# GpSimd writes the scaled states of a tile in one product; start, first norm and last tile rearranged, in a two-layer hybrid decoder step

## The chip, the cores and the metric

The program runs on all 8 cores of one Trainium2 chip, each with its own prompt (2048 tokens) and 16 sample tokens; the weights are the same on each and no core waits for another. The metric is device microseconds of the slowest core.

## What is computed

Per token x (1024 channels), layer by layer, in float32 with bf16 matmul operands:

```
even: h = rmsnorm(x); u,q,f,i,g = h @ w_in          # 256 | 6 heads x 128 each
      pool: mean over 2/4/8/16 tokens - u, per-group linear, scale
      head: k = 1-f, v = silu(i), S_t = diag(f_t) S_(t-1) + k_t outer v_t, o_t = S_t^T q_t
            o = rmsnorm(o) * gain * sigmoid(g)
      x += concat(pool, o) @ w_out
odd:  h = rmsnorm(x); b,c,z = h @ w_in
      x += (b * conv3(c * z)) @ w_out
each: x += relu(rmsnorm(x) @ w1)^2 @ w2              # 4096 wide
end:  y = rmsnorm(x)
```

Outputs are y for the prompt and the samples, and the new states. The recurrence runs by chunks of 128 tokens: with the decay of a chunk as a column, the state before chunk j is scaled by cc[:, j], cast to bf16 and multiplied by the decayed q; a masked product inside the chunk is added.

## The kernel before

Channels lie on partitions, tokens along the free dimension. The 2064 tokens go in two halves (0 to 1023, 1024 to 2063); a half is cut into tiles for the heads (HT: 512 tokens) and for the dense part (DT: 512 in the first half, 352, 352 and 336 in the second). Weights come from DRAM as float32 and are cast to bf16 by the DMA into a ring of six slots of 4096 columns; GpSimd issues these loads (g_load, two DMAs of 2048 columns a unit). x, outputs and states are moved by SyncE's queue.

The program is written as Python generators (g_...), one for each piece of work. A list scheduler (Sched) takes, among the operations that the generators offer, the one with the lowest estimated start plus a small weight times its priority, and appends it to its engine's instruction stream. So the order on each engine is fixed when the program is built; at run time the engines only wait on semaphores. PRI holds the priorities by name, DMA_RATE the transfer speeds that the estimates use. The numbers of the scheduler change only the order.

The pieces that matter here:
- g_x0 loads the first half of x: tile 0 in two parts of 256 columns, two DMAs each, then, when the weights of head 1 have landed, tile 1. Head 0's weights wait for tile 0's second part, head 2's for a part of tile 1.
- g_norm: eight squares (ScalarE), seven adds (VectorE or GpSimd, seng), a matmul with ones (float32, passes=4), Ln and Exp (ScalarE), and eight products into hT (VectorE). With final=True the products go to pages and each is sent out by one DMA (two where the sample tokens are in it).
- g_x1 loads the second half's x for the heads into mixT, used as a staging area, after the first half's fronts.
- g_front(h, t): projections f, i, g of head h on tile t, with their sigmoids. Weights lie as kc * 512 + r * 128 (q, f, i, g). g_back(h, t): log decay, its scan (VectorE), the exponentials, q projection, transposes, the masked product, then the state steps. The last are:

```
for j in range(nj):
    yield ACT(Spb[j], Vin, AF.Copy, ..., scale=cc[:, j:j + 1])       # scaled state, bf16
    yield STT(Vout, Vin, cc[:, j:j + 1], bank(kd_)[j], mult, add)    # V_(j+1) = cc_j V_j + K_j
    yield MMG([(bank(ko)[j], Spb[j], qd[j]), (bank(ko)[j], vtok[j], sm[j])])
    Vin = Vout
```

- g_pools: the pooling mixer, one of whose tiles has adds on GpSimd.
- g_outproj, g_ff1, g_ff2, g_conv: the dense part. The dense part of the first half runs interleaved with the heads of the second half. g_ff2 in its last pair spawns the norm of the next layer, or the final one.
- Each GpSimd tensor product also writes B_poolser, so they run one after the other.

In the profile, L494 is ACT, L514 tensor_tensor (TT), L529 scalar_tensor_tensor (STT), L549 matmul groups, L558 transposes, L564 DMA issue.

## Time and profile before

| | |
|---|---|
| median of three runs | 1538.13 us (1537.94 to 1538.3) |
| profiled execution | 1537.33 us |
| span of its slowest core | 1535.8 us |
| spans of all cores | 1529.1 to 1535.8 us |
| granted TensorE clock, mean | 0.984 |
| TensorE busy | 1455.6 us (95%) |
| VectorE, ScalarE, GpSimd busy | 887.7 (58%), 632.0 (41%), 186.0 us (12%) |
| moved by DMA | 138.56 MB, mean 90 GB/s |

The profile is of the slowest core. "Busy" counts the union of an engine's instructions; the granted clock of a stretch is 1.00 at 2.4 GHz and 0.50 at 1.2 GHz. A releaser ("<-DVE arena L514") is the instruction whose end let a waiting one go. Names as arena, ring, hT, mixT, x_sb are SBUF tensors, pp a PSUM bank. A DMA row of a queue gives packets, megabytes written and the share of 16 DMA engines' time; q0 is GpSimd's queue, q1 SyncE's.

### The profile page before, as it was taken

How to read it: one execution, taken by the hardware profiler on the slowest of the kernel's cores; microseconds unless marked ns; L12 is line 12 of the kernel's file. 1: busy time of each engine (PE TensorE's matmuls, PEld its weight loads, DVE VectorE, ACT ScalarE, POOL GpSimd, SP SyncE). 2: the span in 40 equal slices, each digit the busy share in tenths (PEclk: the TensorE clock that was granted, in tenths of full speed). 3: DMA queues.
4: the chain of work that ended last, by engine and by line, in shares of the span. 5: the costliest groups of instructions: out<-in, count | busy, mean ns of one | idle time of the engine just before them, and what ended most of it. 6: DMA issues, size and time to landing. Idle time of an engine off the chain costs nothing.

```text
span 1535.8 us, 24078 instructions; the slowest of 8 cores (1529.1 to 1535.8 us)
## 1 busy us (share of the span) xinstructions
PE 1455.6 (95%) x9034; PEld 817.6 (53%) x9034; DVE 887.7 (58%) x1860; ACT 632.0 (41%) x1187; POOL 186.0 (12%) x272
## 2 busy tenths in 40 slices
PE   2789799999999999999999999999999999999996
PEld 1445344554555444444444446666666666666663
DVE  4766686676657768565333368533357767433355
ACT  3788747655797433222212234222133224211132
POOL 1233313001111141100100010001001110001000
PEclk9899799999999999999999999999999999999998
DMA  6835333157346646962633558055245544155222
GB/s 142 183 56 83 56 56 85 28 114 166 83 85 140 152 70 99 174 117 52 110 56 61 104 111 167 15 97 85 51 72 83 95 89 83 25 86 95 52 58 75
DMA packets 49553, 138.56 MB, mean 90 GB/s; under 512 B 7840, under 2 KB 15904, under 8 KB 47904
## 3 DMA queue, kind: packets, MB, share of 16 engines
q0 software_dynamic: 29408, 101.76, 39.9%
q1 hardware_dynamic: 19600, 34.93, 6.9%
q8 instruction: 75, 1.23, 0.3%
q10 hardware_dynamic: 432, 0.33, 0.1%
q14 instruction: 38, 0.31, 0.1%
HBM read 223.21 MB, written 15.54 MB: 155 GB/s over the span
## 4 chain that ended last, share of the span: by engine, by line
PE 90%; ACT 4%; DVE 3%; DMA 1%; issue 1%; POOL 0%; DVEq 0%; SPq 0%; ACTq 0%; POOLq 0%
PE pp L549 89%; ACT arena L494 3%; DVE hT L529 1%; ACT L494 1%; DVE arena L514 1%; DMA x_sb<-xp 1%; DMA ring<-wst 1%; DVE arena L529 0%; POOL arena L514 0%; PE pp L558 0%; DVE arena L542 0%; DVE x_sb L514 0%; ACT mixT L494 0%; DVE mixT L514 0%; DVE mixT L529 0%
## 5 line engine op out<-in xcount | busy, mean ns | idle before, releaser
L549 PE MATMUL pp<-hT,ring 128*128 128x512 bf16 (+3 forms) x4320 | 785.5, 339 | 5.4 <-DVE hT L529 4.5
L549 PEld LDWEIGHTS pp<-hT,ring 128*128 128x128 bf16 x4320 | 408.5, 98 | 346.6 <-issue 24.9
L549 PE MATMUL pp<-mixT,ring 128*128 128x512 bf16 (+2 forms) x3200 | 576.0, 339 | 7.5 <-DVE mixT L514 4.5
L549 PEld LDWEIGHTS pp<-mixT,ring 128*128 128x128 bf16 x3200 | 311.4, 98 | 249.8 <-issue 17.1
L494 ACT ACTIVATE mixT<-pp 128x512 bf16<-128x512 f32 (+2 forms) x320 | 164.6, 514 | 485.2 <-PE pp L549 484.3
L514 DVE TENSOR_TENSOR x_sb<-x_sb,pp 128x512 f32<-128x512 f32 (+3 forms) x384 | 220.7, 579 | 199.0 <-PE pp L549 198.6
L514 DVE TENSOR_TENSOR mixT<-mixT 128x512 bf16<-128x512 bf16 (+2 forms) x320 | 119.3, 376 | 234.8 <-ACT mixT L494 233.9
L564 POOL DMA_DIRECT2D ring<-wst x202 | 107.7, 542 | 971.0 <-PE pp L549 957.2
L494 ACT ACTIVATE arena<-pp 128x512 f32<-128x512 f32 (+9 forms) x261 | 129.2, 508 | 160.2 <-PE pp L549 142.7
L494 ACT ACTIVATE arena<-x_sb 128x512 f32<-128x512 f32 (+3 forms) x184 | 97.6, 538 | 156.7 <-DVE x_sb L514 144.3
L514 DVE TENSOR_TENSOR arena<-arena 128x512 f32<-128x512 f32 (+6 forms) x195 | 114.3, 586 | 23.6 <-ACT arena L494 19.6
L514 DVE TENSOR_TENSOR arena<-pp,arena 128x512 bf16<-128x512 f32 (+5 forms) x124 | 75.2, 610 | 76.7 <-ACT arena L494 48.6
L514 POOL TENSOR_TENSOR arena<-arena 128x512 f32<-128x512 f32 (+5 forms) x62 | 76.4, 1232 | 295.8 <-ACT arena L494 116.0
L494 ACT ACT_TABLE_LOAD x71 | 91.1, 1283 | 4.6 <-issue 2.5
L529 DVE SCALAR_TENSOR_TENSOR hT<-x_sb,cst_s,arena 128x512 bf16<-128x512 f32 (+3 forms) x144 | 84.9, 655 | 11.6 <-ACT arena L494 11.6
L494 ACT ACTIVATE arena<-arena 128x512 f32<-128x512 f32 (+3 forms) x128 | 73.0, 585 | 11.3 <-PE pp L549 5.0
L549 PE MATMUL pp<-arena 128*128 128x128 bf16 (+2 forms) x504 | 59.2, 225 | 14.5 <-ACT arena L494 12.0
L529 DVE SCALAR_TENSOR_TENSOR arena<-arena,cst_s 128x512 f32<-128x512 f32 (+4 forms) x88 | 53.2, 608 | 23.1 <-ACT arena L494 21.7
L549 PEld LDWEIGHTS pp<-arena 128*128 128x128 bf16 (+1 forms) x504 | 36.2, 100 | 46.9 <-issue 32.6
L549 PEld LDWEIGHTS pp<-ring,hT 128*128 128x128 bf16 (+1 forms) x816 | 47.7, 98 | 6.8 <-issue 2.9
L549 PE MATMUL pp<-ring,hT 128*128 128x128 bf16 (+1 forms) x816 | 50.5, 220 | 0.0
L494 ACT ACTIVATE arena<-arena,cst_s 128x512 f32<-128x512 f32 (+2 forms) x40 | 25.3, 636 | 57.8 <-DVE arena L514 57.8
(65 smaller groups left out, 426.1 us busy)
## 6 DMA issues: line engine op xcount, KB each, us to landing
ring<-wst POOLq DMA_DIRECT2D x186, 512.0 KB, 9.0
arena<-st_hgrn SPq DMA_DIRECT2D x6, 1024.0 KB, 5.3
nhs<-arena SPq DMA_DIRECT2D x6, 1024.0 KB, 7.4
x_sb<-xp SPq DMA_DIRECT2D x8, 512.0 KB, 10.7
mixT<-xp SPq DMA_DIRECT2D x8, 512.0 KB, 7.8
ring<-wst POOLq DMA_DIRECT2D x16, 256.0 KB, 7.9
yp<-arena SPq DMA_DIRECT2D x16, 256.0 KB, 10.2
yp<-arena SPq DMA_DIRECT2D x16, 176.0 KB, 1.9
```

Source lines behind the costliest of these rows:

```text
L494: return e.activation(out=out, in_=in_, func=func, bias=bias, scale=scale)
L514: return Op(eng, lambda e: e.tensor_tensor(out=out, in0=in0, in1=in1, op=op), R, W, occ=d, dur=d)
L529: return Op("dve", lambda e: e.scalar_tensor_tensor(out=out, in0=in0, scalar=scalar, in1=in1, op0=op0, op1=op1), R, W, occ=d, dur=d)
L549: ins = e.matmul(o, l, r, start=s, stop=t)
L564: fns = [(lambda e, o=o, i=i: e.dma_start(out=o, in_=i, **kw)) for (o, i) in pairs]
```

## The change

1. State steps: the four ScalarE casts become two GpSimd products, one for chunk 0 and one for chunks 1 to 3 behind the third step; the eight matmuls stand together after all four steps.
2. Loads at the start: no gate on any weight load; tile 0's x from a second copy (xp0) in which four channels of 256 tokens are contiguous; head 0's weights in four DMAs of 1024 columns, each with its own buffer name and semaphore; the weights of a head are laid out by projection (f, i, g, q, 1024 columns each). g_x1's loads wait for head 5's weights.
3. First norm (g_normx): tile 0's two parts have a norm of their own. Three of the eight products go ScalarE copy, then GpSimd product; the sum over channels is partly done by accumulating matmuls. Tile 1's adds go to GpSimd. Front (0, 0) runs its projections by half tiles, the first of them chunk by chunk.
4. Last tile: in the last pair of the last g_ff2 the tile of 336 columns is cut at 1952 into 224 and 112. Both get g_norm_tail: adds for channels 1 to 5 only, three squares straight to the matmul, three products on GpSimd, and outputs in four DMAs of two channels, for the last on two queues, and one for the samples.
5. Writes into mixT by second-half heads and pooling wait for the norm of tile 3. "poolp" is set after the sample part.
6. New priorities, seed and DMA rates. JIT is 0, so the seed has no effect.

```
-    PRI = {'norma': 0, 'frontA': 4.6, 'add': 8.7, 'pools': 10.8, 'normy': 59.0, 'cchain': 18.7, 'normc': 0, 'normz': 4.2, 'poolA': 3.1}
-    DMA_RATE = {"sp": 200e3, "act": 200e3, "pool": 270e3}
+    PRI = {'norma': 0, 'frontA': 12.9, 'add': 12.3, 'pools': 10.8, 'normy': 65.5, 'cchain': 17.8, 'normc': 0, 'normz': 18.0, 'poolA': 9.8, 'normp': 12.3, 'poolB': 10.5, 'normb': 7.4, 'relu': 0, 'backB': 20.4}
+    DMA_RATE = {"sp": 300e3, "act": 200e3, "pool": 300e3}
...
+                st = 1024 if key == ("H", 0, 0) else 2048
+                for c0 in range(0, unit_cols[u], st):
...
+                if key[0] == "H":
+                    for i, pr in enumerate(pairs):
+                        k = st // 1024
+                        if key == ("H", 0, 5):
+                            gate_x1.extend(B_ring[s])
+                        yield DMA("pool", ring_ds[s][i * k], [pr], after_, B_ring[s][i * k:(i + 1) * k], nbytes=st * 512)
...
-                        extra = [B_ring[loaded[("H", 0, 1)]]] if t == 1 and q == 0 else []
...
-                if t == 0:
-                    yield WAIT(("ld", ("H", 0, 1)))
...
+                        src = xp0[:, i, cs, :] if t == 0 else xp[:, cs, u:v]
...
+                    if t == 0:
+                        S.spawn(g_normx(u, v), 0, f"normp{u}")
+                    else:
+                        S.spawn(g_norm(0, u, v, *xloc(0, u, v), seng="pool"), 5, f"normx{u}")
...
+        def g_normx(a, b):
...
+            else:
+                for c in range(8):
+                    s_, Bs_ = sq[c % 4]
+                    yield ACT(s_, xap(c), AF.Square, xbf(c), Bs_)
+                    yield MMG([(bank(pk)[:, 0:N], onesf, s_, c == 0, c == 7)], Bs_ + [B_const], [B_ps[pk]], passes=4)
...
+            nx = 3
+            for c in range(nx):
+                yield ACT(xg[c][0], xap(7 - c), AF.Copy, xbf(7 - c) + [B_const], xg[c][1], scale=gcols[:, 7 - c:8 - c])
...
+                if c < nx:
+                    yield TT(hT[:, 7 - c, a:b], xg[c][0], rs, ALU.mult, xg[c][1] + Br, bh(7 - c, a, b), eng="pool")
...
+            yield TT(Spb3[:, 0:1, :], Vc[:, h:h + 1, :], cc3[:, 0:1, :], ALU.mult, [B_V[h]] + Bcc + Blf[0][1:], BSpj[0], eng="pool")
             Vin, BVin = Vc[:, h, :], [B_V[h]]
             for j in range(nj):
                 Vout, BVout = (V3[:, j, :], BVj[j]) if j < nj - 1 else (Vc[:, h, :], [B_V[h]])
-                yield ACT(Spb[:, j * 128:(j + 1) * 128], Vin, AF.Copy, BVin + Bcc + Blf[0][1:], BSpj[j], scale=cc[:, j:j + 1])
                 yield STT(Vout, Vin, cc[:, j:j + 1], bank(kd_)[:, j * 128:(j + 1) * 128], ALU.mult, ALU.add,
                           BVin + Bcc + [B_ps[kd_]] + BG, BVout)
+                Vin, BVin = Vout, BVout
+                if j == nj - 2:
+                    yield TT(Spb3[:, 1:nj, :], V3[:, 0:nj - 1, :], cc3[:, 1:nj, :], ALU.mult, BVj + BG + Bcc, BSpj[1:], eng="pool")
+            for j in range(nj):
                 yield MMG([...])
...
+            if T0 >= SPLIT:
+                yield WAIT(("hT", 0, HT[1][-1][0]))
...
+                tiles = [(a, a, b) for (a, b) in DT[half]]
+                if last and n_after == 4 and half == 1:
+                    ta, tb = DT[1][-1]
+                    tiles[-1:] = [(ta, ta, TCUT), (ta, TCUT, tb)]
...
+            for i, cs in enumerate(((0, 1), (4, 5), (2, 3), (6, 7))):
+                yield DMA(("sp", "act")[i % 2 if b > NT else 0], y_ds[y_ptr[0] % len(y_ds)],
+                          [(yp[:, cs[0]:cs[1] + 1, a:a + e], yo[:, cs[0]:cs[1] + 1, 0:e])], [BO[c] for c in cs], (), nbytes=e * 1024)
...
-        S.spawn(g_load(head_seq(0), Q_HEAD, {("H", 0, 0): (("xl", sum(HT[0][0]) // 2, 0), bx(0, sum(HT[0][0]) // 2, HT[0][0][1])), ("H", 0, 2): (("xl", HT[0][1][0], 1), bx(2, *HT[0][1]))}), 40, "hload")
+        S.spawn(g_load(head_seq(0), Q_HEAD), 40, "hload")
```

## Rows read from the trace of the kernel before

**Rows 1.** The page, part 4: shares of the chain that ended last, by line.

```profile
PE pp L549 89%; ACT arena L494 3%; DVE hT L529 1%; ACT L494 1%; DVE arena L514 1%; DMA x_sb<-xp 1%; DMA ring<-wst 1%; DVE arena L529 0%; POOL arena L514 0%; PE pp L558 0%; DVE arena L542 0%; DVE x_sb L514 0%; ACT mixT L494 0%; DVE mixT L514 0%; DVE mixT L529 0%
```

**Rows 2.** Busy time by stage: start:end, length, busy (x instructions), granted clock, DMA share, GB/s.

```profile
0.00:29.86 29.86, 2.38 (x4) 1.03 (x5) 15.23 (x52) 10.04 (x23) 4.56 (x12) 1.00 0.75 147
...
41.00:60.00 19.00, 12.23 (x53) 5.22 (x51) 12.47 (x23) 15.57 (x28) 5.93 (x9) 0.73 0.99 225
60.00:107.00 47.00, 38.97 (x324) 23.06 (x323) 34.24 (x75) 38.88 (x68) 13.37 (x14) 0.99 0.51 86
107.00:188.00 81.00, 66.75 (x502) 37.45 (x501) 56.39 (x118) 69.33 (x127) 23.47 (x26) 0.88 0.43 66
...
258.00:276.00 18.00, 14.23 (x79) 7.06 (x78) 12.85 (x30) 11.78 (x27) 3.62 (x6) 0.81 0.75 117
276.00:530.00 254.00, 253.08 (x1774) 130.89 (x1773) 167.67 (x345) 167.75 (x310) 26.17 (x39) 1.00 0.48 105
...
1511.70:1521.05 9.35, 9.28 (x64) 6.19 (x64) 6.53 (x14) 3.38 (x7) 0.00 (x0) 1.00 0.22 81
1521.05:1535.80 14.75, 0.80 (x2) 0.30 (x2) 5.36 (x11) 1.42 (x3) 0.00 (x0) 0.68 0.30 93
```

**Rows 3.** Chain, then timeline, 0 to 62 us: start, length, engine, line, operation.

```profile
1.57 11.50 DMA x_sb<-xp
...
18.34 3.25 DVE L529 SCALAR_TENSOR_TENSOR hT<-x_sb,cst_s,arena 128x256 bf16<-128x256 f32 x8
...
26.46 3.25 DVE L529 SCALAR_TENSOR_TENSOR hT<-x_sb,cst_s,arena 128x256 bf16<-128x256 f32 x8 [2.41 <-ACT arena L494]
...
29.86 3.57 PE L549 MATMUL pp<-hT,ring 128*128 128x512 bf16 x8 [4.48 <-DVE hT L529]
...
39.14 1.95 PE L549 MATMUL pp<-ring,hT 128*128 128x128 bf16 x32
...
59.70 0.99 DVE L529 SCALAR_TENSOR_TENSOR hT<-x_sb,cst_s,arena 128x512 bf16<-128x512 f32 x1
```

**Rows 4.** DMA queues in 16:29, 36:46, 903.1:911.1, 607.6:610.3, 676.8:678.2: packets, MB, share.

```profile
q0 software_dynamic: 468, 1.72, 89.0%
...
q1 hardware_dynamic: 1759, 3.39, 92.7%
...
q0 software_dynamic: 275, 1.00, 81.1%
q1 hardware_dynamic: 344, 0.65, 22.8%
...
q0 software_dynamic: 115, 0.33, 81.6%
q1 hardware_dynamic: 146, 0.13, 15.2%
...
q0 software_dynamic: 39, 0.14, 47.9%
q1 hardware_dynamic: 437, 0.12, 38.8%
```

**Rows 5.** GpSimd on arena tiles, whole span: ns min/median/max, first and last.

```profile
L514 POOL TENSOR_TENSOR arena<-arena x62: 1038/1087/2372, 43.5 to 570.8; 128x512 f32<-128x512 f32 x38, 128x526 f32<-128x526 f32 x8, 64x524 f32<-64x524 f32 x4, 128x524 f32<-128x524 f32 x4
```

**Rows 6.** ScalarE, 41 to 188: casts by form; TensorE waiting for it (us, times).

```profile
L494 ACT ACTIVATE arena<-arena,gsm 128x128 bf16<-128x128 f32 x36 | 13.2, 394 | 2.2 <-DVE arena L529 2.1
...
L494 ACT ACTIVATE arena<-Vc,gsm 128x128 bf16<-128x128 f32 x12 | 4.6, 396 | 0.0
...
  PE pp L549: 16.1, 25
```

**Rows 7.** The chain that ended last, 236 to 290 us.

```profile
258.94 11.15 DMA ring<-wst
```

**Rows 8.** Timeline from 1490 us: the last tile's output.

```profile
1524.86 3.92 DVE L529 SCALAR_TENSOR_TENSOR arena<-x_sb,cst_s,arena 128x336 f32<-128x336 f32 x8 [2.16 <-ACT arena L494]
...
1532.73 0.43 SPq L564 DMA_DIRECT2D ys<-arena  x1
```

More of the change, by code:

```diff
@@ L352, in build @@
     xp = din("xp", [128, 8, NT])
+    xp0 = din("xp0", [128, 2, 8, 256])
     xs = din("xs", [128, 8 * NSMP])
@@ L462, in bm @@
             return [Bm_[c][i] for i in segs(TB, a, b)]
-        B_ring = [Buf(f"ring{i}") for i in range(NSLOT)]
+        B_ring = [[Buf(f"ring{i}_{q}") for q in range(4)] for i in range(NSLOT)]
         B_pg = [[Buf(f"pg{i}lo"), Buf(f"pg{i}hi")] for i in range(NPAGE + NOV)]
@@ L655, in g_norm @@
             N = b - a
+            if final and b >= (TCUT if TCUT else NTOK):
+                yield from g_norm_tail(n, a, b, xap, xbf, seng)
+                return
             pA, pS, pT = yield GRAB(1, 1, 1)
@@ L836, in g_front @@
             yield ACT(s1, bank(kf)[:, 0:L], AF.Sigmoid, [B_ps[kf]], Bs1, scale=-1.0)
             hput(kf)
-            (ki,) = yield from htake(half)
-            yield MMG([(bank(ki)[:, j * 128:(j + 1) * 128], hT[:, kc, T0 + j * 128:T0 + (j + 1) * 128], Wt(kc, 256, 384),
-                        kc == 0, kc == 7) for j in range(nj) for kc in range(8)], Rw, [B_ps[ki]])
+            if first:
+                yield proji(ki, Tm, T1, [B_ps[ki], Bx2[ki][1]])
+            else:
+                (ki,) = yield from htake(half)
+                yield proji(ki, T0, T1, [B_ps[ki]])
@@ L844, in g_front @@
             PAGES.put(p3)
-            (kg,) = yield from htake(half)
-            yield MMG([(bank(kg)[:, 0:L], Wt(kc, 384, 512), hT[:, kc, tk], kc == 0, kc == 7) for kc in range(8)], Rw, [B_ps[kg]])
+            if first:
+                yield proj(kg, 2, Tm, T1, [B_ps[kg], Bx2[kg][1]])
+            else:
+                (kg,) = yield from htake(half)
+                yield proj(kg, 2, T0, T1, [B_ps[kg]])
             yield ACT(sg, bank(kg)[:, 0:L], AF.Sigmoid, [B_ps[kg]], Bsg)
```

161 lines of the change are left out of this document (128 added, 33 removed).

## Prediction

> **What bounds the kernel now.** I began with the chain of waits [rows 1]: 89% of the span is TensorE in the one helper that records matmuls, so only time in which TensorE has nothing to do, or works at its lower clock, can be won. The second view is the table of busy time by stage [rows 2]. The reader should subtract TensorE's busy time from each stretch: 27.5 us idle before 29.86, 6.8 in 41 to 60, 8.0 in 60 to 107, 14.3 in 107 to 188, 3.8 in 258 to 276, 0.9 in 276 to 530, 14.0 after 1521.05. These seven make 75.3 of the 80.2 us that TensorE idles in all; the dense work between has nothing to give. The granted clock tells the rest: 0.73 in 41 to 60, 0.88 in 107 to 188, 0.81 in 258 to 276; each fall follows a stretch with gaps. So three places matter: the start, the first half's heads (41 to 188), the end.
>
> **The start: loads.** In before, the first x tile (columns 0 to 511, 2 MB) comes alone; the weights of head 0 wait for it. The critical chain has the second x piece landing at 1.57 + 11.50 = 13.1 us; the first hT chunk begins at 18.34 (5.3 us after it), the second half's eight chunks run 26.46 to 29.71, and the first projection starts at 29.86 [rows 3]. After, every load is issued at once: SyncE sends x tile 0, then x tile 1; GpSimd sends six slots (heads 0 to 4 and pooling), 13 DMAs, with no gate. How 16 DMA engines share between the queues decides. Ring loads alone move 132 GB/s (1.72 MB in 13 us) at a share of 0.89, so 150 GB/s of bf16 at full share [rows 4]: a head (1.05 MB) is 7.0 us of all engines, the six slots 5.8 MB or 38 us. Where both queues were full, 344 packets of 2 KB went beside 275 ring packets, 1.25 to 1 [rows 4]. Pieces of 896 B, strided at both ends, went 146 to 115, or 1.27 to 1. But 64-byte pieces cut from a contiguous source row of 512 B went with 39 ring packets at 437 in all, some 11 to 1 [rows 4]: a turn seems to be a contiguous source run. The new input xp0 makes the source run 4 KB while SBUF is still written in 1 KB pieces, so I take four pieces a turn.
>
> Bounds for x tile 0 (2048 pieces; alone it needs about 8 us of all engines, an estimate: 2.1 MB at some 260 GB/s, between the 147 GB/s of the first stretch in rows 2 and the 339 GB/s of 2 KB pieces in rows 4). At four to one it meets 512 ring packets, just head 0: 8 + 7 = 15 us, landed at about 17. At 1.27 to one it meets 1613 of the 1664: 8 + 37 = 45, landed at about 47. I take the first, since the 64-byte row has the same shape.
>
> The new first norm has the same chain (5.3 us), with five chunks on VectorE and three products on GpSimd instead of eight on VectorE. First half: 1024 pieces beside 256 ring packets, 4 + 3.5 us, landed about 11 with latency, first chunk 16, and TensorE does projections f, i, g of half the tile meanwhile. Second half: landed 17, first chunk 22 to 23, last 25. Against 29.86 this is 5 us, and another 3 for half of the three projections done early (the first eight matmuls take 3.57 us, [rows 3]; three such projections 7 to 10), 8 in all. But then x tile 1 is late next. It follows on the same queue with 2 KB pieces, at 1.25 to one: 1024 pieces beside some 820 ring packets (3.4 MB, 22 us) plus 6 us of its own (2.1 MB at 339 GB/s, [rows 4]) lands about 17 + 28 = 45 to 50. Its norm adds, moved to GpSimd, cost 1.09 us each (GpSimd's median, [rows 5]), in a chain behind the squares: hT of tile 1 from about 56, against 59.70 [rows 3]. So the 8 us shrink to 3. I count -3, with ends -9 (x tile 1 lands early) and +6 (the second end of the sharing, half hidden because the work of tile 1 then follows without a gap).
>
> **State casts.** Per head and tile, before: four ScalarE casts of 128x128 between the state steps; they are 36 + 12 in the first half's heads at 0.39 us, 13.2 + 4.6 = 17.8 us [rows 6]. After: one GpSimd product of 128 columns, one of 384 behind the third step. ScalarE is busy 15.6 of 19, 38.9 of 47 and 69.3 of 81 us [rows 2], 84% of 41 to 188, and TensorE waits 16.1 us, 25 times, for a ScalarE tile there [rows 6], of 29.1 us idle (55%). Upper end: the stretch follows ScalarE, -17.8. Lower end: nothing is freed on the path, and the longer chain is open 12 times. Its length: before, the last cast stands behind step three with 0.39 us; after, the 384-column product does and lasts, by width from 1.04 us (the shortest of 512 columns, [rows 5]), 0.8 us, up to 1.8 by the longest (2.37). I take 1.0, since the median is near the shortest; less the 0.39 of the cast that it replaces, 0.6 us: 12 x 0.6 = +7. My value: 55% of 17.8 = -9.8, plus 0.6 for each of the last two heads, behind which nothing is queued: about -9. Part of this is clock: fewer gaps in 107 to 188, where 0.88 was granted. In the second half, 12 more pairs of products stand beside dense matmuls, with TensorE idle 0.9 us in 254 [rows 2]: cost 0; with the cover gone, +7.
>
> The products wait on VectorE's step, on an in-order queue, and ring loads stand behind them. Before shows what that costs: a load issued only at 258.9, in the middle of norm adds, landed 11.15 us later and was the chain [rows 7], in the stretch with 3.8 us idle and a clock of 0.81, some 6 us in all (14.2 busy x 0.19 = 2.7, plus 3.8). The new priorities reorder this place too, either way: 0, with ends -6 and +6. Of x half 2, moved behind head 5's load, the mixT writes wait for the norm by an explicit WAIT; its readers start beyond 270, so 0.
>
> The Trainium skill's page "SBUF — State Buffer", section "Who interferes with whom", speaks against this change: a VectorE instruction with two SBUF inputs and a GpSimd one that reads SBUF exclude each other for a whole instruction. The trace agrees so far as that equal products on GpSimd take 1.04 to 2.37 us [rows 5]. By it each of the first half's 12 wide products could wait one VectorE instruction of 0.7 us more (an estimate), the whole sum 8 us smaller: 1527, the end of the likeliest case's own range.
>
> **The end.** Before, from 1521.05: add, square, sum, matmul, Ln, Exp to 1524.86; eight chunks, 3.92 us; SyncE issues sixteen DMAs, the last at 1532.73 [rows 8]; 14.75 us in all. After, the last tile is cut at 1952 into 224 and 112 columns. TensorE: 64 matmuls at 336 columns take 9.28 us [rows 2], 145 ns each. 128-column ones take 1.95/32 = 61 ns [rows 3], floor for 112; 224 by width is 98 ns. 64 x (61 + 98) = 10.2, so +0.9. Behind the last matmul, at 112 columns: add 0.3, square 0.35 and matmul 0.4 (the last three squares go to TensorE directly), Ln and Exp 0.8, then five chunks of some 0.27 beside three on GpSimd 1.3, issue 1.0 on two queues, landing 2.5: 6.7. VectorE's backlog from the 224 columns (16 adds, 5 chunks in 3.9 us of matmul) adds some 1.2. 14.75 - 0.9 - 7.9 = -6. Ends: -8 (no backlog), -4 (the two queues land one after the other).
>
> **Sum.** -3 - 9 + 0 - 6 = -18. The profiled run took 1537.3 (span 1535.8 plus 1.5), 0.8 below the median of 1538.1. So 1519.5. The likeliest case's own range: 1511 to 1527.
>
> **Rivals.**
> A. GpSimd takes ScalarE's place. TensorE waits as long for the 384-column product as it did for the casts, so 41 to 188 keeps its length. For it: the chain really is longer, and one wait gates all eight matmuls. Against it: those waits were ScalarE's queue, not only one cast. 1537.3 - 3 + 2 - 6 = 1530.
> B. Head and clock both give. With fewer gaps the clock never falls in 107 to 188 (66.8 busy x 0.12 = 8 us back), x tile 1 lands by 40 (-9). 6 of those 8 beyond the 9 counted: 1537.3 - 9 - 9 - 6 - 6 = 1507. Against: tile 1 needs DMA time that the weights take.
> C. Slower: x starves. If the turn is one 1 KB piece, x tile 0 lands about 47, all second-half chunks at 54 instead of 29.71, +24, less 3 for early projections. Nothing hides it, TensorE has only the first half's projections. 1537.3 + 21 - 9 - 6 = 1543. It decides once more than about 1400 of the 1664 ring packets go ahead of x tile 0's last piece. For it: 2 KB and 896 B rows; against: the 64-byte row. The Trainium skill's page "DMA: Bandwidth & Descriptors", section "Queues, rings and completion order", says that each engine switches queues at packet boundaries and that a packet holds many descriptors; this trace's 2 KB and 896 B rows look like single pieces, and the measurement decides.
> D. It doesn't do what it says: order shifts eat the gain in the heads and only the end is won, with loads held behind GpSimd products: 1537.3 - 6 + 6 = 1537.
>
> **How the numbers follow.** Forecast 0.56, A 0.19, B 0.13, C 0.07, D 0.05. The range reaches from just below B's 1507 to between A and D, and leaves out C, D and what of B lies lower, some 0.17: 1505 to 1536. A measurement of this kernel tells about 0.2%, 3 us. Faster by more: forecast, B, A and a little of D, 0.88; same 0.04; slower 0.08.
>
> **What would show it.** First projection between 15 and 18 us, second half of the tile by 24: the sharing is right; at 45, C. hT of tile 1 from 54 to 58. ScalarE busy in the first heads down by some 18 us, its row of 128x128 casts gone, TensorE's waits for ScalarE in 41 to 188 below 8 us and those for GpSimd below 6 us; above 12, A. The stage that ends at 188 in rows 2 ends about 176. GpSimd's 384-column product near 0.8 to 1.0 us. No new wait on a ring load over 3 us. From last matmul to the end 7 to 9 us. I am wrong if GpSimd's queue holds loads, or if the new order opens gaps between 276 and 1150, of which before shows none.

## The result, and the profile after

The changed kernel takes 1558.78 us (median, 1557.98 to 1561.38) against 1538.22: a ratio of 1.0135, 95% interval 1.0122 to 1.0147, so 20.6 us slower. The forecast was 1519.5, and the range ended at 1536. In some runs, of the kernel before too, a pair of cores or half of the chip shows a lower granted clock than the rest; such runs are left out (e17's interval has one, and with theirs e9 would be at 1560.4 and e12 at 1567.3), and of e1 to e4, where it was so every time, only the other four cores are used.

The page of the kernel after (core 2, span 1556.4 us; in before TensorE was busy as long, 1455.6 us, and the same line had 89% of the chain [rows 1]):

```profile
PE 1455.5 (94%) x9052; PEld 828.2 (53%) x9140; DVE 894.2 (57%) x1851; ACT 604.4 (39%) x1111; POOL 239.0 (15%) x346
...
PE pp L551 84%; DMA x_sb<-xp 3%; ACT arena L496 3%; DMA ring<-wst 2%; ACT L496 2%; SPq L566 1%; DVE arena L516 1%; DVE arena L531 1%; POOL arena L516 1%; DVE hT L531 0%; PE pp L560 0%; ACT mixT L496 0%; DVE mixT L531 0%; POOL ring L566 0%; DVE arena L544 0%
...
x_sb<-xp SPq DMA_DIRECT2D x8, 512.0 KB, 31.2
```

The chain gives DMA 3 and 2% of the span, and the median DMA of x (eight of 512 KB) takes 31.2 us from issue to landing. The stages of core 2, with the columns of [rows 2]:

```profile
0.00:29.86 29.86, 6.61 (x18) 3.73 (x18) 9.81 (x35) 6.78 (x17) 11.66 (x24) 0.94 0.94 180
41.00:60.00 19.00, 0.40 (x1) 0.00 (x0) 4.88 (x5) 5.21 (x11) 7.09 (x7) 0.50 0.69 146
60.00:107.00 47.00, 42.62 (x329) 25.36 (x335) 32.30 (x64) 39.33 (x56) 16.48 (x19) 0.92 0.27 52
107.00:188.00 81.00, 68.31 (x547) 41.28 (x554) 55.27 (x118) 71.04 (x104) 30.47 (x38) 0.92 0.38 63
276.00:530.00 254.00, 246.52 (x1578) 125.85 (x1603) 143.58 (x283) 114.16 (x208) 34.67 (x53) 1.00 0.46 93
```

TensorE idles 23.3 us before 29.86 (27.5 in before), 18.6 in 41 to 60 (6.8), 7.5 in 276 to 530 (0.9). Between the last two the order differs too much to compare by the clock, so I count from the residual adds, of which the first 384 (of 416, of 424 where the last tile is cut) are the same in both kernels; the first marks the start of the first outproj. A stage's loss is TensorE's idle time plus its busy time times (1 - the clock granted while it was busy).

| stage (adds) | before, core 4 | after, core 2 | after, core 4 |
|---|---|---|---|
| start to first add | 191.5, loss 68.7 | 202.0, loss 83.8 | 200.8, loss 82.3 |
| to the 17th | 82.3, 6.4 | 85.2, 7.0 | 83.5, 5.3 |
| to the 113th | 493.9, 2.3 | 509.4, 16.2 | 499.7, 6.8 |
| to the 384th | 678.6, 2.6 | 673.7, 3.2 | 673.7, 3.2 |
| to the end | 89.5 | 86.1 | 84.9 |

So the start loses 10 us where 12 were to be won, and 12 to 16 more go between 290 and 800 us on one core of each pair (0 and 1, 2 and 3, ...), 6 to 7 on the other. The other core is 8 to 14 us faster in every run: the medians are 1553.9 and 1543.6, against 1535.4 and 1530.5 in before. TensorE's waits for ring loads, core 2 and then core 3 (us in all, times, longest), and a piece of core 2's chain:

```profile
PE pp L551 <- DMA ring<-wst: 6.5, 3, 3.8
```

```profile
PE pp L551 <- DMA ring<-wst: 1.3, 2, 1.0
```

```profile
411.84 0.59 POOL ring L566
412.43 20.25 DMA ring<-wst
```

**The start, as it ran.** DMA queues of core 2 from 12 to 32 us (packets, MB, share), the longest piece of its chain before 400 us, then its timeline; a bracket gives the idle time before and what ended it:

```profile
q0 software_dynamic: 1142, 2.51, 75.8%
q1 hardware_dynamic: 1137, 1.29, 27.2%
```

```profile
14.14 43.01 DMA x_sb<-xp
```

```profile
1.07 14.95 SPq L566 DMA_DIRECT2D x_sb<-xp  x8
...
20.79 0.42 PE L551 MATMUL pp<-hT,ring 128*128 128x256 bf16 x1
...
30.30 1.03 ACT L496 ACTIVATE arena<-x_sb 128x256 f32<-128x256 f32 x3 [9.72 <-DMA x_sb<-xp]
...
53.80 0.63 ACT L496 ACTIVATE arena<-x_sb 128x512 f32<-128x512 f32 x1 [5.39 <-DMA x_sb<-xp]
54.33 0.40 ACT L496 ACTIVATE arena<-arena 128x256 f32<-128x256 f32 x1
...
54.77 4.88 DVE L531 SCALAR_TENSOR_TENSOR hT<-x_sb,cst_s,arena 128x256 bf16<-128x256 f32 x5 [34.62 <-ACT arena L496]
...
60.92 2.04 PE L551 MATMUL pp<-arena,cst_s 128*128 128x512 f32 x2 [19.52 <-POOL arena L516]
...
63.34 1.86 PE L551 MATMUL pp<-hT,ring 128*128 128x256 bf16 x8 [0.37 <-POOL hT L516]
```

The two queues went packet for packet, 1142 to 1137. Not all of these are large: counted by size in the trace from 12 us to the landing of x tile 0 at 30.2, GpSimd's queue has 1081 packets, 675 of them ring loads (2 or 4 KB written), 256 of the pooling weights (128 B) and 150 of 4 B, and SyncE's has 1080, of which 946 are x tile 0's pieces of 1 KB and 102 tile 1's of 2 KB. Cores 4 and 5 have 1102 to 1098 and 1104 to 1103. x tile 0's four DMAs landed at 6.3, 12.2, 19.2 and 30.2 us (10.3 to 16.0 in before), x tile 1 at 57.1 (44.8 in before; 45 to 50 in the forecast). That last one is the piece of 43.01 us in the chain. The first matmul on half of tile 0 is at 20.79. The second half's square runs at 30.30 as soon as x is there, but its hT begins at 54.77: ScalarE's queue has the squares of tile 1 ahead of the second half's last two steps, and the Exp (54.33) stands behind a square that waited for x tile 1 (53.80). VectorE waited 34.62 us for it. TensorE has tile 1's sum of squares ahead of its projections (19.52 us of wait), and GpSimd's three products end only at 63.2, so it goes on at 63.34. In before tile 0's hT was complete at 29.7. Tile 1's hT begins at 64.5, against 59.7 in before.

### The profile page after: what moved, and what is told of

Its sections match the earlier page's. It is cut to its first block, busy times and chain, and to the rows that moved or that the text cites. A ratio compares the mean times of both kernels' runs of the same rounds, so it can differ in the third digit from the quotient of the medians.

```text
span 1556.4 us, 24216 instructions; the slowest of 8 cores (1542.2 to 1556.4 us)
## 1 busy us (share of the span) xinstructions
PE 1455.5 (94%) x9052; PEld 828.2 (53%) x9140; DVE 894.2 (57%) x1851; ACT 604.4 (39%) x1111; POOL 239.0 (15%) x346
## 3 DMA queue, kind: packets, MB, share of 16 engines
q8 instruction: 76, 1.25, 0.3%
## 4 chain that ended last, share of the span: by engine, by line
PE 85%; DMA 5%; ACT 5%; DVE 3%; issue 1%; POOL 1%; SPq 1%; DVEq 0%; POOLq 0%; ACTq 0%
PE pp L551 84%; DMA x_sb<-xp 3%; ACT arena L496 3%; DMA ring<-wst 2%; ACT L496 2%; SPq L566 1%; DVE arena L516 1%; DVE arena L531 1%; POOL arena L516 1%; DVE hT L531 0%; PE pp L560 0%; ACT mixT L496 0%; DVE mixT L531 0%; POOL ring L566 0%; DVE arena L544 0%
## 5 line engine op out<-in xcount | busy, mean ns | idle before, releaser
L551 PE MATMUL pp<-hT,ring 128*128 128x512 bf16 (+4 forms) x4282 | 785.6, 339 | 14.5 <-DMA ring<-wst 5.0
L551 PE MATMUL pp<-mixT,ring 128*128 128x512 bf16 (+4 forms) x3234 | 571.9, 336 | 9.1 <-DVE mixT L516 3.4
L516 DVE TENSOR_TENSOR x_sb<-x_sb,pp 128x512 f32<-128x512 f32 (+5 forms) x392 | 222.0, 569 | 214.1 <-PE pp L551 211.4
L496 ACT ACTIVATE arena<-pp 128x512 f32<-128x512 f32 (+10 forms) x262 | 128.4, 507 | 215.0 <-PE pp L551 162.9
L496 ACT ACTIVATE arena<-x_sb 128x512 f32<-128x512 f32 (+5 forms) x190 | 97.8, 524 | 171.4 <-DVE x_sb L516 125.1
L516 POOL TENSOR_TENSOR arena<-arena 128x512 f32<-128x512 f32 (+6 forms) x80 | 88.7, 1108 | 262.5 <-ACT arena L496 139.6
L516 DVE TENSOR_TENSOR arena<-arena 128x512 f32<-128x512 f32 (+7 forms) x178 | 104.2, 586 | 15.1 <-ACT arena L496 11.0
L516 DVE TENSOR_TENSOR arena<-pp,arena 128x512 f32<-128x512 f32 (+5 forms) x124 | 75.1, 609 | 62.7 <-ACT arena L496 37.0
L496 ACT ACTIVATE arena<-arena 128x512 f32<-128x512 f32 (+4 forms) x129 | 72.5, 582 | 25.2 <-PE pp L551 15.2
L551 PE MATMUL pp<-arena,cst_s 128*128 128x512 f32 (+6 forms) x78 | 34.8, 537 | 48.6 <-POOL arena L516 19.5
## 6 DMA issues: line engine op xcount, KB each, us to landing
x_sb<-xp SPq DMA_DIRECT2D x8, 512.0 KB, 31.2
```

The lines of the kernel that those rows point to most:

```text
L496: return e.activation(out=out, in_=in_, func=func, bias=bias, scale=scale)
L516: return Op(eng, lambda e: e.tensor_tensor(out=out, in0=in0, in1=in1, op=op), R, W, occ=d, dur=d)
L551: ins = e.matmul(o, l, r, start=s, stop=t)
```

## The experiments

Times are medians of the runs that count; "pair" gives the slower and the faster core of a pair. In all of these before ran beside (1538.4 to 1539.7).

| | us | ratio, 95% | pair |
|---|---|---|---|
| before | 1538.4 | | 1535.4, 1530.5 |
| e5 after, loads gated, order remade | 1545.5 | 1.0050 (1.0033 to 1.0066) | 1541.9, 1532.2 |
| e6 before + casts + tail | 1540.8 | 1.0018 (1.0008 to 1.0027) | 1536.8, 1529.0 |
| e7 after, ScalarE casts | 1572.4 | 1.0215 (1.020 to 1.023) | 1567.3, 1560.2 |
| e8 after, old priorities and rates | 1554.2 | one run | 1551.1, 1547.1 |
| e9 = e5 + e8, front (0, 0) behind all eight hT chunks | 1553.2, 1554.3 | two runs | |
| e10 = e6, tail on VectorE | 1538.0 | 1.0002 (0.9991 to 1.0012) | 1534.6, 1525.9 |
| e11 = e10, casts of first half only | 1538.9 | 1.0004 (0.9994 to 1.0014) | 1534.1, 1523.7 |
| e12 = e9, x tile 1 early | 1551.9 | one run | |
| e13 = e10, new priorities and rates | 1549.0 | 1.0063 (1.0046 to 1.0081) | 1544.8, 1533.7 |
| e14 = before, new priorities and rates | 1563.2 | one run | 1557.3, 1542.1 |
| e15 = e5, x tile 1 early | 1550.4 | 1.0070 (1.0046 to 1.0095) | 1546.6, 1535.6 |
| e16 after, gates in the same order | 1556.3 | 1.0112 (1.0094 to 1.0129) | 1550.2, 1538.7 |
| e17 = e13, old rates | 1543.1 | 1.0057 (1.0016 to 1.0099) | 1538.7, 1529.5 |
| e18 = e10, new rates | 1562.1 | 1.0153 (1.0138 to 1.0168) | 1559.0, 1546.8 |

**The start: e1, e2, e5, e16.** Two theories: the landing of the loads (S), and the order that the scheduler made in the belief that they land early (O).

```
e1, e16 (after; semaphore waits alone, no engine's order changes)
+        dp[0] += [(x_ds[2].h, 16), (x_ds[3].h, 16)]           # GpSimd's first load: x tile 0, second part
+        dq[4] += [(ring_ds[1][0].h, 16), (ring_ds[1][2].h, 16)]   # SyncE's x tile 1: head 1's weights
+        dp[7] += [(x_ds[5].h, 16)]                            # a later load of GpSimd's: a part of x tile 1
e2 (before; x and ring loads issued without their waits, same order)
+            self.prog.dma(op.eng, op.dsem, op.fn, () if self.is_load(op) else op.reads, op.writes)
e5 (after; the gates of before, known to the scheduler)
+                        extra = B_ring[loaded[("H", 0, 1)]] if t == 1 and q == 0 else []
+                if t == 0:
+                    yield WAIT(("ld", ("H", 0, 1)))
+        S.spawn(g_load(head_seq(0), Q_HEAD, {("H", 0, 0): ..., ("H", 0, 2): ...}), 40, "hload")
```

> The changed kernel with the three load gates of before put back as semaphore waits only: every engine's order of instructions stays that of the changed kernel. Theory S (the ungated weight loads starve x, all of the loss at the start is theirs): first tile's hT complete by 31 us instead of 69, first add of the outproj by 191 instead of 201, total within 4 us of before (1534 to 1542). Theory O (the new order of the engines is the larger part: ScalarE's queue has four squares of tile 1 ahead of the second half's Ln, and ring loads in the dense part come just in time): hT of the first tile only at 45 to 50, since tile 1 still lands at 40 to 45; half of the cores still lose 10 us at ring loads near 410 and 760; total 1545 to 1552.

Measured (core 5): x tile 0 landed at 13.3, yet hT of tile 0 was complete at 58.5, and outproj began at 196.0; on the four cores it was 196.0 to 201.4, against 200.2 to 202.1 in the changed kernel. The slowest of these four took 1556.4 to 1558.6 us, above what either theory gave.

> The kernel before with the three load gates taken away, the order on every engine kept. Theory S: x tile 0 lands at 28 to 31 us instead of 16, tile 1 at 55 to 58 instead of 45; first projection at 37 instead of 29.9; total 6 to 12 us slower (1544 to 1550). Theory O: the first tile is late but the work of tile 1 follows without a gap, total at most 3 us slower.

Measured (core 6): x tile 0 landed at 33.4 (16 in before), first projection 41.8 instead of 29.9. Outproj began at 205.5 to 209.5 on the four cores; in e4, whose start is that of before and which ran beside it, at 191.2 to 195.5, so 14 us later in the mean. The slowest of the four took 1558.0 to 1571.8 us, above both theories. x came here from the old layout, with source runs of 1 KB, but beside other loads than in the changed kernel: only heads 0 and 1 (507 packets of 4 KB by 33.4 us), since the next ring loads stand in GpSimd's queue behind a product at 55.60, and on its own queue x tile 1, in pieces of 2 KB. So e2 doesn't tell what laying four channels together was worth.

> The changed kernel with the three gates of before put back (head 0's weights behind x tile 0, x tile 1 behind head 1's weights, head 2's weights behind a part of x tile 1), and known to the scheduler, so that the engines' order at the start is made anew: the squares of tile 1 no longer stand ahead of the second half's Ln. Theory (the start loses the time, by the loads and by the order made for them): hT of tile 0 complete by about 30 us (69 in the changed kernel), outproj begins at 176 to 182 (200.8), whole kernel 12 to 22 us under the changed kernel, 1537 to 1547. Rival 1 (the loss is of the ring loads that run just in time, on one core of each pair): outproj early, but the loss comes back by 800 us, under 8 us gained in all. Rival 2 (GpSimd's products hold the heads up): outproj still later than 188.

Measured: 1545.5, 13 us under the changed kernel, as the theory had it; but outproj began at 185.7 to 189.9, later than its 176 to 182. (The 69 us in the text on record are those of tile 1's hT; tile 0's was complete at 63.2.) Its timeline on core 3 has the second half's hT at 24.95 and the projections on it at 28.69:

```profile
24.95 3.48 DVE L531 SCALAR_TENSOR_TENSOR hT<-x_sb,cst_s,arena 128x256 bf16<-128x256 f32 x5 [1.63 <-ACT arena L496]
...
28.69 2.59 PE L551 MATMUL pp<-hT,ring 128*128 128x256 bf16 x14 [1.88 <-DVE hT L531]
```

> The changed kernel with the three gates as waits alone, every engine in the changed kernel's order. Theory O (the order made for early loads loses the time, not only their landing): x tile 0 lands by 14 us, but tile 0's second hT half is complete only at 55 to 60, since tile 1's squares stand ahead of its Ln; the whole 1553 to 1559, 0 to 5 us better than the changed kernel. Rival S (the landing alone does it): 1543 to 1548.

Measured: 1556.3, only 2.5 under the changed kernel. Core 5:

```profile
42.50 3.71 POOL L566 DMA_DIRECT2D ring<-wst  x7 [22.69 <-DMA x_sb<-xp]
...
46.16 2.40 POOL L516 TENSOR_TENSOR hT<-arena 128x256 bf16<-128x256 f32 x3
...
48.70 0.37 PE L551 MATMUL pp<-hT,ring 128*128 128x256 bf16 x1 [22.47 <-POOL hT L516]
...
56.57 6.38 DVE L531 SCALAR_TENSOR_TENSOR hT<-x_sb,cst_s,arena 128x256 bf16<-128x256 f32 x5 [39.55 <-ACT arena L496]
```

ScalarE's order holds the Exp as before (VectorE waits 39.55). But the gates themselves stand in GpSimd's queue: its seven ring loads wait 22.69 us for x tile 1, and the three hT products of the first half, behind them, run at 46.16, with TensorE waiting 22.47 for them. So e16 doesn't split the 13 us cleanly between S and O. What the four runs show together: late landing alone costs the start of before some 14 us (e2, same order), and taking it away from the changed kernel brings back 0 to 5 us at outproj and 2.5 in all unless the order of ScalarE, GpSimd and TensorE is made for it (e1, e16 against e5).

**The casts: e3, e6, e7, e10, e11.**

```
e3, e6, e10 (before): the casts as in the change; e6, e10 with the two WAITs of part 5 and the last tile cut
e7 (after)
-            yield TT(Spb3[:, 0:1, :], ..., eng="pool")
-                    yield TT(Spb3[:, 1:nj, :], ..., eng="pool")
+                yield ACT(Spb[j], Vin, AF.Copy, ..., scale=cc[:, j:j + 1])
e11 (e10): the GpSimd products if half == 0, the ScalarE casts if half == 1
```

> The kernel before with the state casts alone done by GpSimd. The prediction's step: 17.8 us of ScalarE work gone from the first heads, TensorE's waits for ScalarE in 41 to 188 down from 16 to under 8 us, total 9 us faster (1529). Theory P (GpSimd takes ScalarE's place, and ring loads stand behind its waits): waits for GpSimd of 8 us or more there, total between 2 us faster and 8 us slower.

Measured: outproj began at 177.2 to 184.4 us on the four cores (191.2 to 195.5 in e4); the 96 adds after the 17th took 505 to 510 instead of 499. The slowest of the four took 1546.1 to 1551.7 us, and before, beside it, 1543.7 to 1557.9: the forecast's 1529 isn't there. (This kernel lacks part 5's WAITs, so a part of the second half's x is overwritten while it is staged in mixT.)

> The changed kernel with the four ScalarE casts back in place of the two GpSimd products, all else as changed. If the casts' move is a gain (theory), this is slower than the changed kernel by 5 to 14 us: 1564 to 1573, with TensorE's waits for ScalarE up. Rival (GpSimd's in-order queue, with products between the ring loads, causes part of the 20 us): this is as fast as the changed kernel or faster, 1545 to 1558, with the waits for ring loads gone on the slow core of each pair.

Measured: 1572.4, 13.6 slower than with the products. TensorE's waits in the whole span, after (core 2) and then e7 (core 3):

```profile
PE pp L551 <- ACT arena L496: 24.7, 16, 6.8
PE pp L551 <- POOL arena L516: 23.3, 6, 19.5
```

```profile
PE pp L551 <- ACT arena L496: 32.1, 28, 6.2
PE pp L551 <- POOL arena L516: 21.3, 1, 21.3
```

In the changed kernel the casts' move is worth more than the 9 us of the forecast, and GpSimd's products are as short as forecast (after, core 2; busy us, mean ns; the shortest of the 384-column ones took 0.83 us, the longest 1.61):

```profile
L516 POOL TENSOR_TENSOR arena<-arena,gsm 128x384 bf16<-128x384 f32 x24 | 22.1, 919 | 68.7 <-DVE arena L531 56.6 <-DVE gsm L516 6.9 <-DVE mixT L531 3.0
L516 POOL TENSOR_TENSOR arena<-Vc,gsm 128x128 bf16<-128x128 f32 x24 | 12.3, 511 | 21.7 <-ACT gsm L496 21.0
```

> The kernel before with two parts of the change alone: the state casts as GpSimd products (with the two WAITs of part 5) and the cut last tile; loads, first norm, priorities and rates as before. The casts alone began outproj 11 to 14 us earlier than before on an undisturbed die and the tail alone gave 0.3. Theory: the gain of the heads is won, some of it given back between 276 and 545 where the new order opens gaps: 1528 to 1534, so 4 to 10 us faster than before. Rival (the products behind the dense stage take all of it back, TensorE waits for GpSimd there): 1537 or more. By the theory TensorE's idle time before outproj falls from 56.5 to about 45 us.

Measured: 1540.8, slightly slower than before. The theory was wrong here, and so was its number for the idle time before outproj: 57.9 us on core 6, not 45, and 51.2 to 57.9 on all cores, against 52.8 to 57.8 in before.

> As the kernel with casts and tail alone (1540.8), but the six products of the two last tiles' norm that ran on GpSimd run on VectorE. In that kernel GpSimd's last product ended at 1530.16 and its DRAIN at 1538.26, 3.5 us behind SyncE's DRAIN at 1534.73. Theory (GpSimd's drain sets the end): VectorE ends up to 1 us later, the end comes at SyncE's drain, and the stretch from the last residual add to the end falls by 2.5 to 3.5 us: 1537.3 to 1538.3. Rival (the drain waits for something else, or VectorE's three more products per tile cost as much): 1540 to 1542.

Measured: 1538.0, the same as before to 0.1%. Here the pair shows what happened: the faster cores gain 4.6 us, the slower ones 0.8. On every core 3.2 or 2.9 of that are the last tile's (89.5 us to 86.3 or 86.6), so the casts alone bring the fast cores some 1.6 us and cost the slow ones 2.4. The stages of core 2 and then core 0 of e10, side by side:

```profile
30.00:60.00 30.00, 21.59 (x133) 11.77 (x131) 16.07 (x28) 17.82 (x28) 7.33 (x11) 0.83 0.90 210
60.00:107.00 47.00, 42.13 (x335) 24.92 (x336) 28.52 (x65) 34.09 (x51) 13.94 (x17) 0.93 0.45 81
107.00:174.00 67.00, 56.60 (x464) 33.75 (x462) 54.01 (x112) 55.98 (x88) 31.31 (x38) 0.95 0.35 64
```

```profile
30.00:60.00 30.00, 21.50 (x142) 11.69 (x143) 18.68 (x33) 19.19 (x30) 7.34 (x11) 0.89 0.95 221
60.00:107.00 47.00, 41.37 (x356) 25.74 (x362) 34.08 (x74) 38.73 (x60) 17.96 (x20) 1.00 0.37 64
107.00:174.00 67.00, 51.36 (x444) 31.89 (x450) 54.00 (x112) 56.56 (x89) 32.73 (x40) 0.97 0.45 79
```

Core 0 keeps a clock of 1.00 and 0.97 in the heads, core 2 gets 0.93 and 0.95. Core 2 had x tile 0 by 15.0 us, x tile 1 by 44.8 and the first six slots by 72.5; core 0 by 13.3, 36.6 and 66.3. Core 2's TensorE met gaps at other places, and its clock fell to 1.2 GHz seven times before outproj, core 0's three times. Core 0 began outproj at 174.3, core 2 at 184.4.

TensorE's waits for ScalarE in the heads, and its busy time there, core 4 of before, core 2 of e10 and core 0 of e10:

```profile
PE pp L549 <- ACT arena L494: 15.3, 23, 1.4
41.00:188.00 147.00, 117.96 (x876) 65.72 (x874) 103.10 (x215) 123.78 (x222) 42.76 (x48) 0.90 0.53 93
```

```profile
PE pp L550 <- ACT arena L495: 7.4, 9, 1.6
41.00:184.00 143.00, 114.98 (x869) 66.30 (x868) 104.72 (x214) 110.25 (x172) 58.63 (x71) 0.89 0.49 94
```

```profile
PE pp L550 <- ACT arena L495: 5.2, 7, 1.4
41.00:174.00 133.00, 105.31 (x852) 63.40 (x866) 103.60 (x212) 107.90 (x168) 56.85 (x71) 0.96 0.49 84
```

ScalarE's waits were halved, but TensorE's idle time as a whole was 29.0 us and is 28.0 and 27.7: waits for VectorE and GpSimd took their place. What the fast core won is its clock (0.96 for 0.90: 4.4 us lost by it instead of 10.4) and work that the new order puts behind the first add. From the 17th to the 113th add e10 then takes 498 to 503 us where before takes 494, with TensorE idle for 8 to 12 us instead of 2 to 5.

> As the last one, but only the first half's heads have their casts on GpSimd; the second half's, which run beside the dense stages, stay on ScalarE. With the casts on GpSimd in both halves outproj began 5 us (slow core of a pair) to 11 us (fast core) earlier than before, and 276 to 545 us took 5 us longer. Theory (the second half's products cost that): the early start is kept, the stretch behind it is again within 2 us of before's 271.6, the whole 1530 to 1535. Rival (the 5 us are first-half work that merely moved behind outproj): 1536 to 1540, stretch still 276 or longer.

Measured: 1538.9. The stretch from the 17th to the 65th add took 272.7 to 284.8 us (275.8 to 278.7 in e10, 271.6 to 272.0 in before), the start 176.2 to 184.1: the second half's products aren't what was lost, the theory falls. TensorE waited 8 to 12 us for ring loads on the slow cores (0.4 to 4.2 us in e10), with the old priorities and rates: a new order alone brings that.

**The end: e4, e6, e10.**

```
e4 (before): TCUT = 1952, g_norm_tail and the cut tile as in the change
e10 (e6), in g_norm_tail
-                        yield TT(yo[:, c, :], pgf(pX[i], N), rs, ALU.mult, ..., eng="pool")
+                        yield TT(yo[:, c, :], pgf(pX[i], N), rs, ALU.mult, ..., eng="dve")
```

> The kernel before with the last tile's change alone; the order of all engines is that of before up to the last tile. The prediction's step: 6 us faster (1532). From the changed kernel's own trace (89.6 us from the last common add to the end before, 84.8 on its undisturbed core): 5 us faster (1533). If the two output queues land one after the other: 3 to 4.

Measured: from the 384th add to the end (what the texts on record call the last one) 89.2 us instead of 89.5, so 0.3 and not 6; in the changed kernel it is 84.9 to 86.1. The timeline shows e6 (core 6, span 1538.5) with its last issue at 1530.94 and nothing behind, and e10 (core 2, span 1534.7) with its last at 1531.40:

```profile
1529.74 0.42 POOL L515 TENSOR_TENSOR arena<-arena 128x112 f32<-128x112 f32 x1
...
1530.42 1.05 ACTq L565 DMA_DIRECT2D yp<-arena  x2
1530.94 0.60 SPq L565 DMA_DIRECT2D ys<-arena  x1
```

```profile
1530.96 0.97 ACTq L565 DMA_DIRECT2D yp<-arena  x2
1531.40 0.60 SPq L565 DMA_DIRECT2D ys<-arena  x1
```

The rest of the span is no busy time. In the trace's records GpSimd's DRAIN at the end of the program runs from 1529.70 to 1538.26 in e6, while SyncE, which waits for all the outputs, is through at 1534.73. In e4 it lasts 8.55 us, in the changed kernel 3.65 (to 1541.19, before SyncE's 1542.34), in e10 8.78, but from 1519.8, so it is hidden; in before (core 4) it is hidden too (1454.0 to 1468.9). e10's last stretch is 86.3 us, 2.9 under e6's, as the theory had it. Why the drain lasts 3.65 in one kernel and 8.6 in another the runs don't tell.

**Priorities and rates: e8, e9, e12 to e15, e17, e18.**

```
e8 (after), e9 (e5), e12 (e9 with x tile 1 gated on head 0's weights, head 1's on x tile 1)
+    PRI = {'norma': 0, 'frontA': 4.6, ...}                # before's
+    DMA_RATE = {"sp": 200e3, "act": 200e3, "pool": 270e3} # before's
e9, e12 also: front (0, 0) waits for all of its first eight hT chunks
-                yield WAIT(("hT", 0, T0, "s"))
+                yield WAIT(("hT", 0, T0))
e13 (e10), e14 (before): both of the change; e17 (e13): DMA_RATE of before; e18 (e10): DMA_RATE of the change
e15 (e5): x tile 1 gated as in e12
```

> The changed kernel with the priorities and DMA rates of before, all else as changed. Theory: the start stays as late as in the changed kernel (x tile 0 lands near 30, hT complete near 69, outproj at about 200), since the loads are still ungated; of the other 5 to 8 us, lost between 276 and 800 us on one core of each pair, part goes: 1550 to 1558. Rival (the priorities are the cause of the late start): outproj by 188 and under 1545. A second rival (the new priorities were needed with the new parts): slower than 1560.

Measured: 1554.2, 4.6 under the changed kernel, outproj as late as there (199.1 to 201.7), ring waits at most 2.0 us. But in this order tile 0's hT was complete at 44.2 to 46.4, not at 63, with x tile 0 landing as late (28.8 to 30.6); tile 1's hT began at 67.6 to 69.2 instead of 64 to 66. So the late second half of tile 0 alone isn't what outproj waits for; x tile 1, landed at 56.5 to 58.2, is as late in both kernels.

> The changed kernel with the gates of before known to the scheduler and with the priorities and DMA rates of before (front (0, 0) also waits for all of its first eight hT chunks). Gates alone gave -13 (1558.8 to 1545.5), old priorities alone about -5, and they act at different places: the start, and the stretch from 276 to 800 us on one core of each pair. Theory (the two causes add): 1538 to 1542, with TensorE's waits for ring loads below 2.5 us on every core. Rival (with the start repaired the ring loads are as late with any priorities): 1544 to 1548, ring waits of 5 to 8 us on the slow core of each pair.

Measured: 1553.2 and 1554.3. The two gains don't add: outproj began at 181 to 186 us, earlier than in e5, but the next 16 adds took 94 to 96 us instead of 82 to 86, with this wait in 181 to 276 (core 3):

```profile
PE pp L551 <- DVE mixT L531: 6.3, 1, 6.3
```

A half of the first outproj's input waits for one VectorE product that this order puts late. Neither theory had that. With the old numbers, then, the gates bring the whole nothing (1554.2 in e8), though outproj begins some 17 us earlier.

> As the kernel with gates and old priorities, but x tile 1 comes right behind head 0's weights, and head 1's weights behind its first pieces. x tile 1 would land near 36 instead of 44 us. Theory (tile 1's hT, begun at 60 us, is what TensorE waits for at the start): its hT begins 5 to 10 us earlier and outproj 3 to 8 us earlier than in that kernel. Rival (head 1's weights are then late, or ScalarE and VectorE set tile 1's hT): outproj no earlier, the whole within 2 us or slower.

Measured: 1551.9; tile 1's hT began at 50.3 to 56.4 us (59.5 to 61.5 in e9), outproj at 173.6 to 182.1 (181.1 to 186.2); the end moved by 2.

> The changed kernel with gates known to the scheduler, x tile 1 right behind head 0's weights and head 1's weights behind its first pieces. With tile 1 behind head 1's weights it took 1545.5 and outproj began at 186 to 188 us, tile 1's hT at 61 to 63. Theory: hT of tile 1 from 50 to 55 us, outproj 5 us or more earlier, the whole 1538 to 1542. Rival (another engine sets the heads' pace by then): outproj within 2 us of 186 to 188, the whole 1544 to 1548.

Measured: 1550.4. Outproj at 175.1 to 179.1, some 11 us before e5, and the whole 4.9 slower than e5: TensorE waits 14 to 16 us for ring loads on the slow cores. The start's gain is real and is lost behind it.

> The kernel before with the casts, the tail (all its products on VectorE) and the new priorities and rates; loads and first norm as before. The same with old priorities took 1538.4, the changed kernel with gates put back (new priorities, new first norm) 1545.5. Theory P (the new priorities cost the 7 us): 1543 to 1550. Theory N (the new first norm does): 1535 to 1540.

> The kernel before with the new priorities and rates alone (and part 5's WAITs, without which the order deadlocks). Theory P: 1543 to 1550. Theory N: 1536 to 1541. If the priorities were good only together with the casts, this one is slow (over 1543) and the one with casts is not.

Measured: 1549.0 and 1563.2. Theory P holds in its direction: on the start of before the new numbers cost 11 us with the casts and some 24 without, 13 more than its range had.

> Casts and tail with the new priorities but the DMA rates of before (with new rates 1549.0, with both old 1538.4). Theory R (the rates, which promise loads earlier than they land, cause the ring waits): 1536 to 1542, ring waits under 5 us on all cores. Theory Q (the priorities do): 1545 to 1552, ring waits of 5 to 12 us as with the new rates.

> Casts and tail with the old priorities and the new DMA rates. Theory R: 1544 to 1552 with ring waits above 5 us. Theory Q: 1536 to 1541, ring waits as with the old rates (0.4 to 4.2 us). If both this and the run before are over 1543, any order other than the one that before was tuned to costs about as much.

Measured: 1543.1 and 1562.1. The first is just outside theory R, the second 10 us above its range, with the ring waits on R's side in both. Of four kernels that differ only in priorities and rates:

| | old rates | new rates |
|---|---|---|
| old priorities | 1538.0, ring waits 0.4 to 4.2 us | 1562.1, 7.9 to 17.8 |
| new priorities | 1543.1, 0 to 6.7 | 1549.0, 5.3 to 12.3 |

The rates cost 24 and 5 to 6 us, the priorities 5 on the old rates; on the new rates the new priorities bring 13. TensorE's waits for ring loads follow the rates. They are the smaller part of the 24: e18 begins outproj at 190 to 196 us where e10 does at 174 to 184. Both runs are over 1543, the sign that was named for a third reading, that any order costs about as much but the one that the old numbers were tuned to. No run here excludes it. e10 and then e18, core 7, whole span, and a late piece of e18's chain:

```profile
PE pp L550 <- DMA ring<-wst: 4.2, 3, 2.2
```

```profile
PE pp L550 <- DMA ring<-wst: 16.8, 5, 4.8
```

```profile
543.52 21.23 DMA ring<-wst
```

## Why the prediction was wrong

1. **The sharing of the queues** is the step that failed first. The text took four pieces a turn for x against the weights because one row with 64-byte pieces looked so [rows 4]; it let 512 ring packets go beside x tile 0, landed at 17 us. Measured, with source runs of 4 KB: one for one, 1080 packets to 1081, so a turn isn't a source run. x tile 0 landed at 30.2, and 932 ring packets had gone; the 420 beyond 512 are of 4 KB, 1.72 MB, 11.5 us at the text's own 150 GB/s (an estimate), most of the 13. The 1.25 and 1.27 to one of the 2 KB and 896 B rows, set aside, were the nearer ones. Rival C had the direction; its own sign, 1400 ring packets, wasn't reached, its 47 us were too late (the first 12 us went 1134 to 280), and its 1543 too low, because it took the landing to be the whole. x tile 1 then landed at 57.1, not 45 to 50. The Trainium skill's page "DMA: Bandwidth & Descriptors", section "Queues, rings and completion order", has queues switch at packets of many descriptors. The trace gives totals, 1081 to 1080, and not how many of one queue go in a row, so it neither confirms nor refutes that.
2. **What stands in the queues behind a late load** was not asked. The text let the second half's chain of 5.3 us run as soon as its x landed. It ran 24.6 us late (30.2 to 54.8), behind tile 1's squares in ScalarE's queue. The order is written by the scheduler from estimated landings; if these are wrong, the order is. e5 against after prices landing and order together at 13.3 us, where I had -3 for the start (ends -9 and +6). That price belongs to the new priorities and rates: with the old ones it is under 1 us (e8 against e9).
3. **The new priorities and rates**, put at "0, with ends -6 and +6", are the second large miss. e13 against e10: +11, and e14 against before some +24. Rows of before suggest why the rates matter: [rows 4] has ring loads at 132 GB/s of bf16, which is 264 GB/s of the float32 that DMA_RATE counts, and x tile 1 took 9.9 us (core 3) and 12.1 (core 2) for 2.1 MB, 212 and 173 GB/s. The old numbers, 270 and 200, are close to these (though at full pace pieces of x moved at 339 GB/s [rows 4]); the new, 300 and 300, promise the landings 14% (ring) and 40 to 70% (x) faster. I had both rows and didn't set them against the line of the diff. That the rates and not only the priorities do it is shown for two orders (e17, e18); that it is through this mismatch is argued. Nor are the new numbers worse everywhere: they cost 11 us on e10 and 4.6 on the changed kernel (e8), and with gates they are 8 faster (e5 against e9, which differs in one more WAIT).
4. **State casts:** the sign holds in the changed kernel only, and the mechanism not even there as it was written. Forecast -9; e7 against after 13.6; but on the base of before +2.8, since of e10's 0.4 us the last tile's part is 3.2. The text took 55% of ScalarE's freed time to be won because that share of TensorE's idle time was a wait for ScalarE. Those waits fell from 15.3 to 7.4 us (e10, core 2) and those for GpSimd are 4.2, as asked for, yet the idle time in the heads stayed (29.0 and 28.0): that is rival A's mechanism with VectorE beside GpSimd. And the second half's products, priced at 0, came with 5 to 9 us more between the 17th and the 113th add; e11 says it isn't the products themselves. The exclusion of VectorE and GpSimd, put at 0.7 us a product, isn't seen at that size: 0.92 us in the mean against 0.83 for the shortest; and the 2.37 us that the text read as an equal product's is of one of 64 partitions, the longest of 128x512 took 1.53. The metric takes the slowest of eight cores. I read [rows 2] from one core, the slowest, and took its clock of 0.88 as given; the spans of the eight cores, 1529.1 to 1535.8, were in the table and unexplained.
5. **The end:** -6 forecast, -3.4 on the slowest core and -4.6 on the others. The backlog was undersized, and GpSimd's drain, which no step had, took nearly the whole of it in e4 and e6.
6. **Nothing in 276 to 1150** would change, I said, and named the opposite as what would prove me wrong. 7.5 us idle there instead of 0.9 in 276 to 530.

The account from before to after, by kernels: casts and tail -0.4 (e10), new priorities and rates +11 (e13), first norm, head loads in four and the tail's products on GpSimd -3.5 (e5), no gates and the order made for that +13 (after): 1538.4 to 1558.8. It holds for this path; points 2 and 3 show that on another the same steps have other prices. No kernel run here beats before by more than can be measured. Open: why one core of each pair loses, and why the same rates cost 24 us in one order and 6 in another. In before, e10, e13, e17 and e18 it is in all four pairs the one whose first loads land later, by 2 to 4 us (before, cores 2 and 3: x tile 0 by 16.1 and 14.0, head 1's weights by 31.8 and 28.1); in the changed kernel it is the other one in three pairs of four (x tile 1 on cores 2 and 3: 57.1 and 58.0). It changes from run to run; what the pair shares, no run tells.

## What to carry to other kernels

Before ungating loads, write down for each in-order queue what stands behind the one that lands last; and where a scheduler orders by estimated transfer times, check its rates against the trace, because an optimistic rate can move work ahead of its data, at the start and as small waits hundreds of microseconds later. Read a change to such numbers as a change to every stage, not as zero. Don't count a wait as won because its releaser has less to do: look at what would end the wait next. Where the time is that of the slowest of several cores, look at how far they stand apart first: a gain that the slow one doesn't share isn't there.

## What the runs showed of the hardware

- Two DMA queues that both had work went packet for packet in one stretch, with packets of mixed sizes: 1080 (946 of 1 KB, 102 of 2 KB, 32 of 4 B) beside 1081 (420 of 4 KB, 255 of 2 KB, 256 of 128 B, 150 of 4 B) from 12 to 30.2 us, and the source runs of the 1 KB pieces were 4 KB. In before, pieces of 2 KB went 344 to 275 [rows 4].
- GpSimd's closing DRAIN lasted 3.65 us in the changed kernel, 8.55 to 8.78 in e4, e6 and e10, and 14.9 in before; it set the end in e4 and e6, whose last GpSimd product ended 8.3 us before it.
- The two cores of a pair differ by 5 us in before (median of the pairs) and by 4 (e8) to 12 (e16) in the variants, single pairs by up to 15, and which one is slow changes from run to run.
- GpSimd's 384-column product with a bf16 output took 0.92 us in the mean, its 128-column one 0.51.
